# Attention in a two-part network: 64-row key and value operands padded to 128 rows, and the next query unit issued ahead of a head group's last steps

## What is computed

```
proj = h @ w_in                          # 2048 -> 5120: c_val c_glu c_gate q k v a_gate r_x r_gate
q, k = partial_rotary(q), partial_rotary(k)           # 16 query heads, 4 key heads, width 64
s    = [q k_meta^T | q k_band^T] / 8     # band: own and previous block of 128, masked to 128 back
p    = softmax([s | sink])               # meta queries see meta keys, causally
att  = p_meta v_meta + p_band v_band ;  y_attn = att * silu(a_gate)
y_conv = (LN+silu of a 31-tap conv of c_val*sigmoid(c_glu)) @ conv_pw * silu(c_gate)
y_lru  = RG-LRU(4-tap conv of r_x) * silu(r_gate)     # a scan along the tokens
h    = layer_norm(alpha * h + [y_conv, y_attn, y_lru] @ w_out)
```

## Time and profile before

| | us |
|---|---|
| median of 3 runs | 3670.15 |
| lowest, highest | 3664.99, 3671.04 |
| span of the profiled execution | 3673.4 |
| TensorE busy in it | 3485.5 |
| VectorE, ScalarE, GpSimd busy | 1734.5, 1270.7, 381.1 |

### The profile page before, as it was taken

The page is one execution under the profiler, slowest core; times in us unless marked ns, Lnnn a source line. Parts: engine busy times, 40 slices in busy tenths (PEclk is TensorE's granted clock), DMA queues, the critical chain, the costliest instruction groups (busy, mean ns, idle before and its releaser), DMA issues.

```text
span 3673.4 us, 58802 instructions
## 1 busy us (share of the span) xinstructions
PE 3485.5 (95%) x22078; PEld 3066.3 (83%) x22078; DVE 1734.5 (47%) x2245; ACT 1270.7 (35%) x1829; POOL 381.1 (10%) x368
## 2 busy tenths in 40 slices
PE   6999999999999998999699999999969999999996
PEld 5888888888888887888498888889959888888995
DVE  5333333443434444246734554555473455455645
ACT  3333332333333333232233343344222434434422
POOL 2000000000000000000303123120030321312002
PEclk9999999999999999999899999999979999999997
DMA  5332233323223323222141221214214112121421
GB/s 175 92 91 91 91 91 97 96 77 97 84 86 92 97 81 132 91 92 91 57 145 53 71 62 55 70 55 137 89 55 140 58 59 70 52 65 58 139 91 46
DMA packets 347354, 319.07 MB, mean 87 GB/s; under 512 B 19040, under 2 KB 339576, under 8 KB 345280
## 3 DMA queue, kind: packets, MB, share of 16 engines
q1 hardware_dynamic: 340224, 283.25, 25.0%
q10 hardware_dynamic: 2592, 19.18, 1.3%
q0 software_dynamic: 4400, 14.62, 1.2%
HBM read 297.74 MB, written 17.07 MB: 86 GB/s over the span
## 4 chain that ended last, share of the span: by engine, by line
PE 53%; DVE 3%; issue 2%; ACT 1%; ACTq 1%; DMA 0%; DVEq 0%
PE ps L512 14%; PE ps L513 14%; PE ps L514 14%; PE ps L781 1%; PE ps L739 1%; PE ps L743 1%; PE ps L783 1%; DVE residual L1543 1%; PE ps L784 1%; PE ps L684 1%; PE ps L763 1%; PE ps L726 1%; ACTq L1086 1%; PE ps L742 1%; PE ps L518 1%
## 5 line engine op out<-in xcount | busy, mean ns | idle before, releaser
L512 PE MATMUL ps<-x_high,w_high 128*128 128x264 f32 (+1 forms) x5280 | 1731.8, 328 | 76.1 <-DVE x_low L1549 53.9
L513 PE MATMUL ps<-x_low,w_high 128*128 128x264 f32 (+1 forms) x5280 | 1709.4, 324 | 9.1 <-issue 9.1
L514 PE MATMUL ps<-x_high,w_low 128*128 128x264 f32 (+1 forms) x5280 | 1704.8, 323 | 0.0
L1276 DVE TENSOR_TENSOR w_low<-w_raw,w_high 128x1024 fp32r<-128x1024 f32 x524 | 655.6, 1258 | 1206.2 <-ACT w_high L890 1165.4
L512 PEld LDWEIGHTS ps<-x_high,w_high 128*128 128x128 f32 x5280 | 1002.4, 190 | 177.2 <-DVE x_low L1549 53.5
L514 PEld LDWEIGHTS ps<-x_high,w_low 128*128 128x128 f32 x5280 | 1000.1, 189 | 87.5 <-issue 9.6
L513 PEld LDWEIGHTS ps<-x_low,w_high 128*128 128x128 f32 x5280 | 1002.9, 190 | 81.0 <-issue 1.9
L890 ACT ACTIVATE w_high<-w_raw 128x1024 fp32r<-128x1024 f32 x524 | 552.2, 1058 | 787.0 <-PE ps L514 671.3
L518 PE MATMUL ps<-w_high,x_high 128*128 128x256 f32 x1184 | 333.7, 282 | 2.0 <-ACT w_spatial_rowsum L937 2.0
L520 PE MATMUL ps<-w_low,x_high 128*128 128x256 f32 x1184 | 334.1, 282 | 0.0
L519 PE MATMUL ps<-w_high,x_low 128*128 128x256 f32 x1184 | 334.0, 282 | 0.0
(11 more groups left out here) (322 smaller groups left out, 2731.3 us busy)
## 6 DMA issues: line engine op xcount, KB each, us to landing
w_raw<-in_w_in SPq DMA_DIRECT2D x776, 256.0 KB, 3.0
w_raw<-in_w_out SPq DMA_DIRECT2D x256, 256.0 KB, 2.8
residual_stream<-y_layer ACTq DMA_DIRECT2D x2, 4224.0 KB, 13.3
residual<-residual_stream ACTq DMA_DIRECT2D x8, 1056.0 KB, 11.0
x_natural<-in_x SPq DMA_DIRECT2D x4, 1024.0 KB, 8.9
x_feature_major<-x_stage POOLq DMA_DIRECT2D x16, 256.0 KB, 4.3
gate_bc<-gate_rows POOLq DMA_DIRECT2D x8, 512.0 KB, 4.4
acc<-x_feature_major POOLq DMA_DIRECT2D x1, 4096.0 KB, 13.7
```

Source lines behind the costliest of these rows:

```text
L512: pe.matmul(dst, wh[:, j, kt, wc], xh[:, k, tok], start=first, stop=False)
L513: pe.matmul(dst, wh[:, j, kt, wc], xl[:, k, tok], start=False, stop=False)
L514: return pe.matmul(dst, wl[:, j, kt, wc], xh[:, k, tok], start=False, stop=last)
L1276: dve.tensor_tensor(wl[:, j], raw[:, j], f(wh[:, j]), ALU.subtract).then_inc(lo_ready, 1)
```

## The change

- Keys are rotated once a layer: `rotate_k` after the first pass of the v unit, and VectorE's rope for the two key tiles in place. The 8 DMAs into `krd` go, with the wait ahead of them on SP's queue.
- `kz` holds the key of the group twice, on the upper and on the lower 64 partitions, the other half being zeros, and for each block the meta keys and the two blocks of the band side by side. A score is one matmul with 128 rows, the query tile of two heads as the stationary operand. ScalarE fills it with 12 copies a group (`keys`).
- `vz` holds v with 64 columns of zeros at each side. `value(i)` is now a whole head at once: 4 matmuls into all 128 partitions, odd heads adding to even ones. The weights of the meta keys of two heads lie on partitions 0 to 15 and 32 to 47 of `y2`'s own attention rows, and one matmul with `vm` adds their part for 512 tokens. `turned` makes one copy more for them. The transposed blocks of a head are kept for 7 x 128 columns, in two buffers.
- Meta queries are a block of the same `pb` tile, read and scaled on 128 partitions.
- `unit(V + 4)`, the next group's query unit, is issued in the group, with `step(21)`, `step(22)`, `recur(0)`, `recur(1)` as hooks of its steps 0 to 3. The first query unit of a layer stands ahead of the loop. The last group stands behind a loop over three, and its V + 4 is the first C_GATE unit with `c_mean` at n = 6 as before.
- ScalarE evacuates the last unit's second half with Silu ahead of the recurrence gates, which come after all of the group's `turned`. Its loop runs over two pairs of groups. The second gate is kept in `y2`'s recurrence row.

```diff
-        qg = rr.take("q_group", [P, 2, L])
-        kg = rr.take("k_group", [P, L])
-        vgr = rr.take("v_group", [P, ST + 1, HD])
+        kz = rr.take("k_zero_padded", [P, 2, 3, NM + 2 * BLK])
+        vz = rr.take("v_zero_padded", [P, ST, 3 * HD])
+        vm = rr.take("v_meta_pair", [P, P])
+        pt0 = rr.take("p_transposed_even", [P, 7 * BLK])
...
-        pb = rw.take("p_block", [P, 2, 4 * (NM + 2 * BLK) + NM])
-        pts = rw.take("p_transposed", [P, 2, 3 * BLK])
+        P1, PW = 2 * NM + BLK, 2 * NM + BLK + 3 * (NM + 2 * BLK)
+        pb = rw.take("p_block", [P, 2, PW])
+        pts = (pt0, rw.take("p_transposed_odd", [P, 7 * BLK]))
...
-                sp.wait_ge(evac, 2 * (U + O_K) + 2)
-                for g in range(NKV):
-                    for o in (0, HD):
-                        s0 = g % 2 * HD
-                        sp.dma_start(krd[o:o + HD, g, :], krw[s0:s0 + HD, g // 2, :]).then_inc(krd_in, 16)
...
+                def rotate_k():
+                    pe.wait_ge(evac, 2 * (U + O_K) + 2)
+                    pe.wait_ge(shape_in, 16 * (l + 1))
+                    pe.wait_ge(pl_ok, l + 1)
+                    for t in range(2):
+                        for q in range(2):
+                            last = pe.matmul(ps[:, 4 + 2 * t + q, 0:LH], rot, krw[:, t, q * LH:(q + 1) * LH], start=True, stop=True)
+                        last.then_inc(rotk_mm, 1)
                 unit_tokens(U + O_V, fill, 0, [
                     [(ps[:, i // 2, i % 2 * 256:(i % 2 + 1) * 256], NM + i * P) for i in range(ST)],
-                    [(ps[:, 2, 0:256], 0)]])
-                with pe.Fori(0, NKV) as g:
+                    [(ps[:, 2, 0:256], 0)]], after=(rotate_k, None))
+                unit(U + O_GRP, fill, wide=True)
...
+                def group(g, ending=None):
...
                     def score(i, n):
-                        o = i % 2 * HD
-                        q = qg[o:o + HD, i // 2, :]
+                        q = qrw[:, i // 2, :]
                         bank = 4 + n % 2
                         if n == 0 and i == 0:
-                            pe.wait_ge(rope_done, 3 * G + 3)
+                            pe.wait_ge(rope_done, 2 * G + 2)
+                            pe.wait_ge(kz_ready, G + 1)
                         pe.wait_ge(s_taken, 4 * A + 4 * i + n + 1)
                         tq = NM + n * BLK
-                        if n < 2:
-                            last = pe.matmul(ps[:, bank, 0:NM + (n + 1) * BLK], q[:, tq:tq + BLK],
-                                             kg[o:o + HD, 0:NM + (n + 1) * BLK], start=True, stop=True)
-                        else:
-                            pe.matmul(ps[:, bank, 0:NM], q[:, tq:tq + BLK], kg[o:o + HD, 0:NM], start=True, stop=True)
-                            last = pe.matmul(ps[:, bank, NM:NM + 2 * BLK], q[:, tq:tq + BLK],
-                                             kg[o:o + HD, tq - BLK:tq + BLK], start=True, stop=True)
+                        w = NM + (2 if n else 1) * BLK
+                        last = pe.matmul(ps[:, bank, 0:w], q[:, tq:tq + BLK], kz[:, i % 2, max(n - 1, 0), 0:w],
+                                         start=True, stop=True)
                         if n == 0:
-                            last = pe.matmul(ps[0:NM, bank, 160:160 + NM], q[:, 0:NM], kg[o:o + HD, 0:NM],
+                            last = pe.matmul(ps[:, bank, 160:160 + NM], q[:, 0:BLK], kz[:, i % 2, 0, 0:NM],
                                              start=True, stop=True)
                         last.then_inc(s_done, 1)
...
-                        if n == 1:
-                            if i == 0:
-                                pe.wait_ge(vgr_ready, G + 1)
-                            o = i % 2 * HD
-                            pe.matmul(ps[o:o + HD, 6, 3 * BLK + 2 * NM:3 * BLK + 3 * NM], vgr[0:NM, 0, :], ptm[:],
-                                      start=True, stop=True)
-                        c0 = n * (NM + 2 * BLK)
-                        pe.transpose(ps[0:NM, 6, 0:BLK], pb[:, i % 2, c0:c0 + NM], ident[:])
+                        if n == 1 and i == 2:
+                            meta_queries(0)
+                        c0 = NM if n == 0 else P1 + (n - 1) * (NM + 2 * BLK)
+                        pe.transpose(ps[:, 6, 0:BLK], pb[:, i % 2, c0:c0 + BLK], ident[:])
                         if n > 0:
                             pe.transpose(ps[:, 6, BLK:2 * BLK], pb[:, i % 2, c0 + NM:c0 + NM + BLK], ident[:])
                             c0 += BLK
                         last = pe.transpose(ps[:, 6, 2 * BLK:3 * BLK], pb[:, i % 2, c0 + NM:c0 + NM + BLK], ident[:])
                         if n == 0:
-                            cm = 4 * (NM + 2 * BLK)
-                            last = pe.transpose(ps[0:NM, 6, 3 * BLK:3 * BLK + NM], pb[0:NM, i % 2, cm:cm + NM],
-                                                ident[0:NM, 0:NM])
+                            last = pe.matmul(ps[:, 6, 3 * BLK:3 * BLK + NM], pb[:, i % 2, 0:BLK], ident[:, 0:NM],
+                                             start=True, stop=True)
                         last.then_inc(pt_done, 1)
...
-                    def value(i, n):
-                        o = i % 2 * HD
-                        if n == 0 and i % 2 == 0:
-                            pe.wait_ge(o_taken, 2 * G + i // 2)
-                        pe.wait_ge(pt_evac, 4 * A + 4 * i + n + 1)
-                        dst = ps[o:o + HD, 7, n * BLK:(n + 1) * BLK]
-                        pe.matmul(dst, vgr[0:NM, 0, :], pts[0:NM, n % 2, 0:BLK], start=True, stop=False)
-                        if n > 0:
-                            pe.matmul(dst, vgr[:, n, :], pts[:, n % 2, BLK:2 * BLK], start=False, stop=False)
-                        last = pe.matmul(dst, vgr[:, n + 1, :], pts[:, n % 2, 2 * BLK:3 * BLK], start=False, stop=True)
-                        if n == 3:
-                            last.then_inc(pv_done, 1)
+                    def meta_queries(c):
+                        y = y2[:, ds(Y_ATT + 2 * g + c, 1), S:S + NM].squeeze(1)
+                        return pe.matmul(ps[:, 6, 3 * BLK + 2 * NM:3 * BLK + 3 * NM], vm[:], y, start=True, stop=True)
+                    def value(i):
+                        c = i // 2
+                        if i % 2 == 0:
+                            pe.wait_ge(o_taken, 2 * G + c)
+                        if i == 0:
+                            pe.wait_ge(vz_ready, G + 1)
+                        pe.wait_ge(pt_evac, 4 * A + 4 * i + 4)
+                        v0 = 0 if i % 2 else HD
+                        for b in range(ST):
+                            e = min(b + 2, ST)
+                            last = pe.matmul(ps[:, 7, b * BLK:e * BLK], vz[:, b, v0:v0 + P],
+                                             pts[i % 2][:, 2 * b * BLK:(b + e) * BLK], start=(i % 2 == 0 and b == 0),
+                                             stop=False, skip_group_check=True)
+                        if i == 3:
+                            meta_queries(1)
+                        if i % 2:
+                            y = y2[:, ds(Y_ATT + 2 * g + c, 1), 0:S].squeeze(1)
+                            last = pe.matmul(ps[:, 7, :], vm[:], y, start=False, stop=True, skip_group_check=True)
+                        last.then_inc(pv_done, 1)
                     def step(k):
                         if k < 4 * GROUP:
                             score(k // 4, k % 4)
-                        if 7 <= k < 7 + 4 * GROUP:
-                            value((k - 7) // 4, (k - 7) % 4)
+                        if k >= 10 and k % 4 == 2:
+                            value((k - 10) // 4)
...
+                    def tail(n):
+                        if n < 2:
+                            step(21 + n)
+                        elif n < 4:
+                            recur(n - 2)
+                        elif ending:
+                            ending(n)
                     unit(V + 1, fill, wide=True, hook=behind(8))
                     unit(V + 2, fill, wide=True, hook=behind(16))
                     unit(V + 3, fill, wide=True, hook=behind(24))
-                    recur(0)
-                    step(21)
-                    step(22)
-                    recur(1)
-                def c_mean():
+                    unit(V + 4, fill, wide=True, hook=tail)
...
-                unit(U + O_CG, fill, wide=True, hook=lambda n: c_mean() if n == 6 else None)
+                with pe.Fori(0, NKV - 1) as g:
+                    group(g)
+                group(NKV - 1, c_mean)
                 unit(U + O_CG + 1, fill, wide=True, hook=lambda n: c_var() if n == 0 else None)
...
+                    def keys(h):
+                        k = krw[s * HD:(s + 1) * HD, ds(gp, 1), :].squeeze(1)
+                        z = kz[h * HD:(h + 1) * HD, h]
+                        for e in range(3):
+                            act.activation(z[:, e, NM:], k[:, NM + e * BLK:NM + (e + 2) * BLK], ACT.Copy)
```

(76 more changed lines are left out.)

87 lines of the change are left out of this document (39 added, 48 removed).

## The result

The changed kernel takes 3614.02 us (median of 4 runs, 3613.2 to 3614.53), the one before 3670.6 in the same measurement: ratio 0.9843, 95% interval 0.983 to 0.9856, that is 57 us faster. The forecast was 3608. The profiled execution has a span of 3612.9 us against 3673.4, 60.5 less.

What follows compares the result with a forecast made beforehand. TensorE, busy 95% of the span, was taken as the bound. Six periods -59.6, two layer ends -6.4 and key rotation +3.6 gave -62.4 us; off the median that is 3608 us, range 3572 to 3645.

Steps and rivals of the forecast that it cites:

- Bursts: TensorE's attention matmuls between weight matmuls: 25.2 us a group instead of 40.7, 15.5 us less.
- 2nd rival: Height isn't the reason: 10.7 of the 15.5 us a group stay, giving 3694 us, slower; chance 0.08.
- surcharge: Extra TensorE time of 64-row float32 matmuls: 272 columns take 0.65 us, expected to fall to 0.46 at full height.
- Seam: Start of the unit after each next query unit: TensorE waits 8.9 us for VectorE's low pieces, covering the jump's idle pieces.
- Tanh behind Sigmoid: On ScalarE at the gates: costed at nothing, or a table load of 1.28 us eight times, +10.
- Clock: TensorE behind each long wait: a slow clock loses 1.9 us, own range 0 to 4 a wait.
- Layer end: Mean matmuls in the C_GATE unit wait 10.5 us for VectorE's add; net -3.2 us, twice, -6.4.
- The period: Time between rotations of successive groups on TensorE: 129.7 us instead of 139.6, 9.9 less, six times, -59.6.
- The key rotation: Once a layer in the value unit: 4 matmuls, 1.78 us, +3.6 us in all.
- ScalarE's copies: New copies for keys, values and transposed blocks: about 5 us, lying in ScalarE's idle time, costed at nothing.
- wait for GpSimd's block: TensorE's first transposes of a group wait for GpSimd's normalized block: +0.9 us a group.
- rival 4: The seam isn't a wait because low pieces come early: -135 us, 3535 us; chance 0.07.

Runs made afterwards that it cites:

- experiment 9: Changed kernel with VectorE's taps ahead of the chain and earlier recurrence gates, plus TensorE's loop over three groups written out: 3521.19 us, ratio 0.9589.
- experiment 4: Changed kernel with score matmuls reading only the 64 rows of their own head, same columns and number of matmuls: 3646.43 us, ratio 0.9933.
- experiment 8: Changed kernel with a 64-column stationary operand in the value matmuls, each head writing its own 64 partitions: 3627.53 us, ratio 0.9873.
- experiment 1: Changed kernel with VectorE's taps 22 to 30 and the add into y_layer moved ahead of or beside the recurrence's products: 3546.05 us, ratio 0.9658.
- experiment 2: Changed kernel with the move undone (query unit at the loop's top, steps and recurrence behind unit V + 3), full height kept: 3591.6 us, ratio 0.9783.

## Why the prediction was right

**Bursts.** 15.5 us a group was the claim. The third period of experiment 9 has no jump and one wait of 0.94 us: 2285.16 - 2166.24 = 118.92, where the prediction's matmuls and that wait make 118.0 + 0.9 = 118.9. So 92.8 + 25.2 was right, and with the 133.5 of before the saving is 15.5 us. Where the 2nd rival would have the surcharge stay, the trace has 0.46 us for 272 columns, and experiment 4 brings 0.65 back with nothing changed but the rows of the scores: 32 us of the whole kernel. What the prediction had wrong is what the surcharge belongs to. It read 0.65 against 0.46 us as the price of 64 rows; experiments 4 and 8 show it as the price of going from one operand size to another. Padding to 128 rows pays here because everything around the scores has 128 rows. The rule of the Trainium skill ("TensorE: Matmul & The Clock Gate", section "Why this matters for your kernels") that a matmul with few rows takes as long as a full one isn't refuted by this, though the prediction says that the trace disagrees: in experiment 4 the starts of a 64-row matmul behind another are 0.12 us apart, as at full height. So the 2nd rival's ground held (the surcharge has another cause) and its conclusion didn't (it went with the small operands).

**Seam.** Forecast 8.9 us of idleness, released by VectorE's low piece; measured 8.40 to 8.44, six times. The chain was 21.06 us from R instead of 21.4. Taking nine taps and the add out of it (experiment 1) removed it: nothing is left at the third seam of a layer, 1.6 to 3.0 us at the others, put down to ScalarE or to issue. Tanh behind Sigmoid needed no load, which also is what the Trainium skill ("ScalarE: Activation LUTs", section "Table sets: the hidden batching unit") says.

**Clock.** 1.9 us a wait was too little: 2.4 us at a seam (5.4 instead of 3.0 for 24 matmuls) and 3.0 at the mean matmuls. At the seams this error and that of the wait cancel: 8.9 + 1.9 was put, 8.4 + 2.4 came, 10.8 both times. That is luck. And a slow stretch at a seam wasn't new: behind the second seam of the kernel before the granted clock was 0.66 over 10 us, behind its first, whose idle pieces the prediction read, 1.00.

**Layer end.** Forecast 10.5 us of wait, 10.2 measured. The stretch to the mean matmuls is 5.2 us shorter; 3.0 are given back in the slow matmuls, so -2.2 instead of -3.2 (its terms add up to -3.3).

**Rest.** The period came out at 129.9 and 130.0 for 129.7; six of them save 58.0 instead of 59.6 us. The key rotation shows as 1.8 us in layer 1, as forecast: from the weight matmul that ends TensorE's wait for the layer's norm (at 1836.36, in the kernel before at 1836.53) to the first rotation of q it is 92.54 us, before 90.74. ScalarE's copies stayed hidden: three of 64 x 256 took 1.03 us and three of 16 columns 0.41, 2.9 us a group for the keys, and VectorE was the one to wait for. The 0.94 us wait for GpSimd's block came as worked out. By the spans of the two traces the change is 60.5 us, by the terms 62.4: they are 2 us off. The other 4 of the 6 us between 3608 and 3614 lie in no term: the span of the profiled execution is 2.8 us above the median time for the kernel before, and 1.1 us below it for the changed one.

**What the prediction didn't see.** It called the move part of one change and never priced the move against leaving it out. Of the 135 us of rival 4, waits and slow clock at seams and ends took more than half, and the move alone is a loss of 66 us. With full height it costs 22 us, some 20 of them at the layer ends. At the seams it is even: the serial tail of experiment 2 waits 0.8, 1.1 and 0.9 us for ScalarE and 2.8 + 2.1 at the jump, and the last two have no work beside them. That the jump's idle pieces rose from a mean of 3.6 us (3.0 to 4.2 over six seams of the kernel before) to 4.9 is shown but not explained.

## What to carry to other kernels

When work of a late stage is tucked under the next stage's matmuls, count what hangs behind it on every other engine, down to the first thing that the stage after needs: here the tucked matmuls were 1.8 us, and what hung behind them 21. If the engine that is late had been idle just ahead of the chain, as VectorE was for 8.5 us, put its independent work there before anything else; that alone was worth more than the whole change. And price the parts of a change one by one: two parts of opposite sign can look like one modest gain. For small matmuls laid between full ones, count the changes of operand size, not the small matmuls.

## What the runs showed of the hardware

- A single float32 matmul with 64 rows between full ones costs 0.40 us more than one with 128 rows and the same 272 columns; two 64-row matmuls in a row cost 0.30 more together, and between them the starts are as at full height (experiment 4). The weight load, which starts 0.12 us ahead of its matmul between operands of one size, starts together with it where the number of rows changes. A burst with 64-column outputs between full ones costs 0.30 to 0.34 us more, and inside it the starts are as at full width (experiment 8).
- Each jump back in TensorE's queue cost about 3.5 us (experiment 9: 14 us for four). In the kernel before and in experiment 2 it shows as two idle pieces, one at the jump and one a little later (13 matmuls later in the one, 4 in the other). Where TensorE waits for VectorE behind the jump, as at the seams of the changed kernel, neither piece shows.
- After 8.4 to 10.2 us of idleness TensorE runs near 1.2 GHz for the next 5.4 to 7 us (granted clock 0.51 and 0.55), and extra matmuls that fill the wait prevent it. Shorter idleness can do it too, but not each time: with pieces of 1.90 and 1.09 us at the second seam of the kernel before the clock was 0.66 over 10 us, with 2.23 and 1.97 us at its first it stayed at 1.00.
